# SwiGLU gate and up products, split by row tile for the first two feature tiles of each layer

## The reference

```python
def swiglu_ffn(x, norm_g, w_gu, w_down):
    h = rms_norm(x, norm_g)
    gate, up = jnp.split(h @ w_gu, 2, axis=-1)
    return (jax.nn.silu(gate) * up) @ w_down

for layer in range(2):
    x = x + mixer(x)            # time mix in layer 0, attention in layer 1
    x = x + swiglu_ffn(x, f_norm_g[layer], f_w_gu[layer], f_w_down[layer])
```

## Time and profile before

| | before |
|---|---|
| runs, us | 1009.56, 1006.28, 1007.12 (median 1007.12) |
| the profiled execution's own time, us | 1006.95 |
| its span, us | 1005.2 |
| TensorE (PE) busy | 968.5 us, 96% |
| VectorE (DVE) busy | 674.3 us, 67% |
| ScalarE (ACT) busy | 432.8 us, 43% |
| GpSimd (POOL) busy | 84.7 us, 8% |

### The profile page before, as it was taken

The page is one execution under the profiler, slowest core; times in us unless marked ns, Lnnn a source line. Parts: engine busy times, 40 slices in busy tenths (PEclk is TensorE's granted clock), DMA queues, the critical chain, the costliest instruction groups (busy, mean ns, idle before and its releaser), DMA issues.

```text
span 1005.2 us, 17451 instructions
## 1 busy us (share of the span) xinstructions
PE 968.5 (96%) x6680; PEld 821.1 (82%) x6680; DVE 674.3 (67%) x1230; ACT 432.8 (43%) x677; POOL 84.7 (8%) x66
## 2 busy tenths in 40 slices
PE   5989999999999999999998999999999999999998
PEld 4868678686788888888897999999998578888887
DVE  6873955748756666666587888788877347666664
ACT  3312313114225444444345656566655434444442
POOL 0101000000010000000021121122112000000000
PEclk9999999999999999999999999999999999999999
DMA  9310310501413766666457545445554127666661
GB/s 303 125 55 2 125 56 1 168 13 46 123 43 94 220 188 188 188 188 188 131 203 220 149 136 157 126 138 147 155 150 126 42 63 197 188 186 189 188 187 55
DMA packets 194836, 136.89 MB, mean 136 GB/s; under 512 B 7246, under 2 KB 185934, under 8 KB 194652
## 3 DMA queue, kind: packets, MB, share of 16 engines
q1 hardware_dynamic: 194780, 136.10, 46.2%
HBM read 135.03 MB, written 1.05 MB: 135 GB/s over the span
## 4 chain that ended last, share of the span: by engine, by line
PE 82%; DVE 11%; issue 2%; DMA 2%; ACT 2%; SPq 0%; POOL 0%; POOLq 0%; ACTq 0%; DVEq 0%
PE bank L408 46%; PE wide L408 33%; DVE work L1137 2%; DVE work L1134 2%; DMA ring<-in_w_kv 2%; PE wide L803 1%; DVE x L1134 1%; DVE work L1356 1%; DVE work L1348 1%; DVE work L1340 1%; ACT work L870 1%; DVE wpj L1134 1%; DMA x<-in_x 0%; PE bank L803 0%; DVE wsp L1134 0%
## 5 line engine op out<-in xcount | busy, mean ns | idle before, releaser
L408 PE MATMUL bank<-wpj,hkq 128*128 128x384 f32 x1152 | 214.5, 339 | 1.8 <-ACT once L870 1.2
L408 PEld LDWEIGHTS bank<-wpj,hkq 128*128 128x128 f32 x1152 | 197.8, 188 | 7.2 <-issue 5.2
L408 PE MATMUL wide<-hsp,wsp 128*128 128x512 f32 (+1 forms) x1056 | 193.0, 339 | 1.4 <-DVE hsp L1134 1.4
L408 PEld LDWEIGHTS wide<-hsp,wsp 128*128 128x128 f32 x1056 | 164.4, 188 | 27.4 <-DVE hsp L1134 1.7
L1134 DVE TENSOR_TENSOR wsp<-ring,wsp 128x1024 fp32r<-128x1024 f32 (+1 forms) x88 | 150.7, 1752 | 3.5 <-ACT wsp L870 3.5
L870 ACT ACTIVATE wsp<-ring 128x1024 fp32r<-128x1024 f32 (+1 forms) x88 | 130.5, 1484 | 19.7 <-PE wide L408 13.8
L408 PE MATMUL bank<-wsp,asp 128*128 128x512 f32 x396 | 98.1, 392 | 0.0
L1134 DVE TENSOR_TENSOR wpj<-ring,wpj 128x1536 fp32r<-128x1536 f32 x48 | 84.2, 1754 | 18.9 <-ACT wpj L870 18.7
L1585 POOL TENSOR_TENSOR gsm<-gsm,mhalf 128x6 f32<-128x6 f32 (+1 forms) x40 | 63.5, 1653 | 307.7 <-DVE gsm L1524 214.8
L408 PEld LDWEIGHTS bank<-wsp,asp 128*128 128x128 f32 x396 | 71.3, 188 | 15.2
L870 ACT ACTIVATE wpj<-ring 128x1536 fp32r<-128x1536 f32 x48 | 71.2, 1484 | 28.8 <-PE bank L408 20.6
(11 more groups left out here) (175 smaller groups left out, 1128.9 us busy)
## 6 DMA issues: line engine op xcount, KB each, us to landing
ring<-in_f_w_gu SPq DMA_DIRECT2D x88, 512.0 KB, 5.9
ring<-in_w_kv SPq DMA_DIRECT2D x96, 256.0 KB, 3.5
ring<-in_f_w_down SPq DMA_DIRECT2D x44, 512.0 KB, 3.8
ring<-in_b_w_q SPq DMA_DIRECT2D x48, 256.0 KB, 3.6
wmix<-in_a_w_k SPq DMA_DIRECT2D x4, 1024.0 KB, 7.7
wmix<-in_a_w_r SPq DMA_DIRECT2D x4, 1024.0 KB, 10.2
wmix<-in_a_w_v SPq DMA_DIRECT2D x4, 1024.0 KB, 5.4
wmix<-in_a_w_o SPq DMA_DIRECT2D x4, 1024.0 KB, 5.3
```

What stands on the lines that cost most here:

```text
L408: return pe.matmul(o, a, b, start=start, stop=stop)
```

## The change: row tile by row tile at both entries

For f = 0 and f = 1 of each layer `gate_up` is replaced by `gate_up_rows(f, b, r)`, which makes gate and up for the 128 rows of one row tile: 16 matmuls of the high weights with both parts of these rows (2 pieces of 128 columns), then 16 of the low weights with the high part (128 columns). Each row tile loads all weights again. The order is (0, r0), (1, r0), (0, r1), (1, r1); each call waits only for its row tile's parts, and `pe_gu` is counted at r1 alone. The transposes of row tile 1 move between the calls. ScalarE and VectorE in layer 0 split row tile 0 before they square and normalise row tile 1, and VectorE makes gu_lo(1) before it splits row tile 1. The fillers become shorter, and the last quarter of the attention's output goes to bank 2 in place of 4.

```diff
-        OUT_BANKS = (0, 1, 3, 4)
+        OUT_BANKS = (0, 1, 3, 2)
...
             product_o(NGRP, [1], 1)
-            keep_clock(14, 4)
+            keep_clock(2, 4)
 
             def ffn(layer):
                 base = layer * NF
-                if layer > 0:
-                    keep_clock(16, 5)
-                turn_rows((fhn, "dve_hn"), RT * layer, range(layer, RT))
-                keep_clock(4, 6)
-                pe.wait_ge(S("dve_hsp"), 4 * (layer + 1))
+                if layer == 0:
+                    turn_rows((fhn, "dve_hn"), 0, [0])
+                    keep_clock(6, 6)
...
+                def gate_up_rows(f, b, r):
+
+                    cut = slice(r * P, (r + 1) * P)
+                    pe.wait_ge(S("dve_hsp"), 4 * layer + 2 * r + 2)
+                    pe.wait_ge(S("act_gu_hi"), f + (base + 1))
+                    for m_ in range(2):
+                        o = gu_bank(b, m_).rearrange("p (s t) -> p s t", s=2)[:, :, cut]
+                        for k in range(KT):
+                            mm(o, gus[b][:, 0, k, m_, :], hparts[:, :, k, cut], k == 0, False)
+                    pe.wait_ge(S("dve_gu_lo"), f + (base + 1))
+                    for m_ in range(2):
+                        for k in range(KT):
+                            m = mm(gu_bank(b, m_)[:, cut], gus[b][:, 1, k, m_, :], hparts[:, 0, k, cut], False, k == KT - 1)
+                        if r == RT - 1:
+                            m.then_inc(S("pe_gu"), 1)
...
-                gate_up(0, 0, False)
-                gate_up(1, 1, False)
+                gate_up_rows(0, 0, 0)
+                if layer == 0:
+                    turn_rows((fhn, "dve_hn"), 0, [1])
+                gate_up_rows(1, 1, 0)
+                if layer > 0:
+                    turn_rows((fhn, "dve_hn"), RT, [1])
+                    keep_clock(5, 1)
+                gate_up_rows(0, 0, 1)
+                gate_up_rows(1, 1, 1)
                 down(0, 0, first=True)
                 gate_up(2, 0)
                 down(1, 1)
...
                 if layer == 0:
                     gu_hi(1, 1, n0 + 1)
-                    squares(1, squared[:, :], "dve_xadd", 4 * NGRP - 4)
+                    squares(1, squared[:, :], "dve_xadd", 4 * NGRP - 4, [0])
                     rows_hi(0)
+                    squares(1, squared[:, :], "dve_xadd", 4 * NGRP - 4, [1])
                     rows_hi(1)
...
                 if layer == 0:
                     norm(1, fhn, "dve_hn", 1, 16, [0])
                     add_output(NGRP, [2, 3])
+                    rows_lo(0)
                     norm(1, fhn, "dve_hn", 1, 16, [1])
-                    rows_lo(0)
+                    gu_lo(1, 1, base)
                     rows_lo(1)
-                    gu_lo(1, 1, base)
                     dn_lo(0, 0, base)
```

## The result

| | before | after |
|---|---|---|
| median of 12 runs, us | 1008.16 (1005.15 to 1009.56) | 1011.01 (1007.06 to 1013.98) |
| ratio | | 1.0030, 95% interval 1.0017 to 1.0042 |
| profiled execution, us | 1006.95 | 1011.30 |
| its span, us | 1005.2 | 1009.6 |

The changed kernel is slower by 0.30%; 1010.3 was forecast. In two later comparisons, on two different chips, the same kernel stood at 1.0055 (1.0040 to 1.0070) and 1.0043 (1.0026 to 1.0059) of the kernel before. So the cost is real, and in both of these it is above the 3.3 us of the forecast.

A forecast was written before the change was run, and what follows sets the result against it. TensorE was taken as the bound, busy 96% of the span at full clock. Entry costs of +2.3 us (layer 0) and +1.0 (layer 1) gave +3.3 on 1006.95, so 1010.3 us; full range 1007.3 to 1021.5.

The forecast's parts named there:

- likeliest case: Weight loads set the slots of the new matmuls: 1010.3 us, own range 1009 to 1012, chance 0.57.
- Slots and pass: Gate and up of one tile, one row tile: 16 high matmuls at 0.119 and 16 low at 0.111, 3.68 us.
- slow fp32r rival: 128-column fp32r matmuls cost as much as plain f32, 0.222 us; pass 5.46, together +13.9, 1020.9 us; chance 0.27.
- hiding one: Rival: weight loads hide under low matmuls, slot 0.06, pass 2.86 us; together −1.7, 1005.2 us; chance 0.13.
- Layer 0: First SwiGLU entry: first pass starts near 304.0, 3.9 us earlier; down starts at 321.6, +2.3 us.
- the square's delay: Layer 0: ScalarE copies tile 0 before squaring tile 1, so the square starts 1.4 us late, hidden by the first pass.
- D0: From the last output product's first matmul to layer 0's first down product; the forecast for this entry was +2.3 us.
- Layer 1: Second SwiGLU entry: first pass starts at 809.70, third ends at 823.4, down starts at 829.05 against 828.05, +1.0 us.
- D1: From row tile 0's first transpose to layer 1's first down product; the forecast for this entry was +1.0 us.
- closing count: Layer 1: 6.95 us of lead eaten by 3.3 of loads, 2.67 of turn, 1.9 of wait, less 0.3 of slack.
- the 0.3 us of slack: Before the change, the down product's wait for tile 0's SwiGLU product was within 0.3 us of being visible.
- What is late next: Behind tile 0, copy, conversion, table load, silu and split product take 5.55 us; one pass covers 3.68, TensorE waits 1.9.

The follow-up runs named there:

- the kernel with the high weights first: Against the kernel before: only high weights' matmuls go row tile by row tile, low weights run once over 256 rows; 1004.77 us against 1006.90, ratio 0.9976.

## Why the prediction was right

*The sign and the size.* Forecast 1010.3, measured 1011.01, within the likeliest case's own range. The steps, in the distances of the profile:

- **Slots and pass.** Taken 0.119 and 0.111 us, pass 3.68; measured about 0.12 and 0.109, pass 3.74. The narrow low matmuls, which the kernel before did not have, cost the weight load: half the columns saved nothing, and weights of half the width took 0.061. The slow fp32r rival (0.222) is out, and so is the hiding one (below 0.08). The Trainium skill ("TensorE: Matmul & The Clock Gate", "Back-to-back issue gap") states about 81 ns for 128 columns; the trace has 0.109 us. (The sum by that figure, given as about +0.2, comes to +0.4, an estimate, with the forecast's own 96 slots: 3.3 − 96 × 0.030.)
- **Layer 0.** From the transposes to the first pass 2.61 us (2.56 forecast); the square's delay is 1.1 us, not 1.4, and hidden either way; D0 +2.11 against +2.3.
- **Layer 1.** From the transposes of row tile 0 to those of row tile 1 15.10 us, as forecast (817.06 − 801.96); D1 +0.81 against +1.0. The forecast's closing count for this entry does not add up to its own +1.0: 3.3 + 2.67 + 1.9 − 6.95 is 0.9, with 0.1 for restarts 1.0, and the 0.3 us of slack does not come off again. The times from which the sum was made are right.
- **What is late next.** The wait for the chain behind tile 0 was put at 1.9 us and is 1.55 at both entries. Tile 0 is complete at about 311.06 + 3.74 = 314.80 and the down product starts at 320.18, 5.4 us later, not 5.65 (5.55 and 0.1 for the restart); by this both sums were 0.2 us high. The rest of the difference is the pass of 3.74 in place of 3.68, and that the 1.55 is counted from the modelled end of the last matmul, about 0.1 us behind its slot.

*What the forecast lacked.* It had 3.3 us of path; the path is 2.9, and 1.4 to 1.6 us come from the granted clock, at layer 1 alone. I named the idle but priced it only as idle. So there is luck in how near the number came: the first measurement gave +2.85 us (1011.01 − 1008.16), less than the 4.4 that its own profiles show, while the later comparisons gave +5.3 and +4.3. The sign and the path are borne out; the size lacks the clock. The three ratios (1.0030, 1.0043, 1.0055) lie around the 2.9 + 1.5 = 4.4 us, or 1.0044, of the profiles; the first of them is the lowest, and its kernel before also ran slowest (1008.16 against 1006.6 to 1006.9). That the same 1.55 us idle lowered the clock at layer 0 in only one of the four profiles that have it there (the one with half of the low columns) isn't explained. Neither the 1.41 us wait at layer 1 in the kernel with the high weights first nor its 1.54 us before the transposes lowered it. So the length of the idle alone does not decide, and what does isn't shown.

## What to carry to other kernels

Splitting a product's moving side to start earlier pays its weight loads twice, so split only what fits into the hole that is there. Split the part whose second load costs least, and leave the rest whole. Here that is the high part: one matmul of 512 columns (0.358 − 0.12 = 0.24 us) becomes two of 256 at 0.12, which costs nothing, while a low one of 256 columns at 0.12 becomes two of 128 at 0.109, nearly double. Then look at what the next consumer of the first part needs: a chain on other engines that the unsplit work just covered becomes the wait. And an idle of TensorE can have two prices, its length and the clock behind it.

## What was not expected of the hardware

After TensorE had stood still for 1.55 us at the entry of layer 1, the granted clock was at 1.2 GHz under the next down product: its 12 matmuls took 4.22 to 4.45 us in the five profiles with that wait, and 2.75 to 2.90 in the eight others. Filler in place of the idle kept the clock at 2.4 GHz in both profiles that have it. The same idle at layer 0 did it in one profile of four.

A table load of 1.28 us moved off the path with a one-element activation of the same function, placed where ScalarE is idle: it stands at 308.26 in place of 317.18 (1.4 us less at each entry of the changed kernel). The copies and the conversion between it and the real silu loaded no other table.
